# An even spread of the retention tiles over mixed weight chunks, and the rotation moved to VectorE

## What is computed

```python
h = rmsnorm(x, g_pre); proj = h @ w_in              # 1024 x 6144: q, k, v, gate
q = rope(q, pos); k = rope(k, pos) * 128 ** -0.5    # 8 heads: q, k of 128, v of 256
scores = einsum(q, k) * inner_dec; inner = scores @ v
R = R * g_c + (k * zeta).T @ v; cross = (q @ R) * xi  # a state carried along the tokens
o = group_norm(inner + cross) * gn_gain
y = (silu(gate) * o) @ w_out; out = x + rmsnorm(y, g_post)
```

## Time and profile before

| | us |
|---|---|
| median of 3 runs (2574.51 to 2578.9) | 2576.57 |
| the profiled execution | 2579.79 |
| its span | 2578.0 |
| first chunks 0 and 1 (14 products), from the start | 143.57 |
| end of the last projection product | 682.40 |
| first matmul of closing tile 2 | 799.41 |

### The profile page before, as it was taken

How to read it: one execution, slowest core, us unless ns; L and a number is a source line. 1 busy time by engine, 2 the same in 40 slices (tenths; PEclk the granted TensorE clock), 3 DMA queues, 4 the chain that set the end, 5 groups by cost and what they waited for, 6 DMA issues and landing times.

```text
span 2578.0 us, 33119 instructions
## 1 busy us (share of the span) xinstructions
PE 2416.0 (94%) x11720; PEld 2026.0 (79%) x11720; DVE 1634.3 (63%) x2643; ACT 1037.8 (40%) x1886; POOL 870.1 (34%) x764
## 2 busy tenths in 40 slices
PE   5599989998778999999999999999999999999999
PEld 4478777777656889878888888888888888888887
DVE  7344777888553244117776577867748766687775
ACT  3454433433331134245555454544434333333332
POOL 4647665665532222062222100110115232342212
PEclk8799999999888999999999999999999999999999
DMA  4333344433645351212233411112242443654422
GB/s 172 111 128 101 115 121 133 130 116 102 181 118 173 125 159 59 93 47 74 67 102 103 152 58 39 53 46 66 78 139 83 179 173 135 241 212 163 164 98 82
DMA packets 157131, 302.17 MB, mean 117 GB/s; under 512 B 13681, under 2 KB 83441, under 8 KB 155761
## 3 DMA queue, kind: packets, MB, share of 16 engines
q1 hardware_dynamic: 156976, 300.18, 35.1%
HBM read 207.07 MB, written 88.87 MB: 115 GB/s over the span
## 4 chain that ended last, share of the span: by engine, by line
PE 71%; DVE 13%; issue 6%; ACT 4%; DMA 2%; POOL 2%; SPq 1%; DVEq 0%; ACTq 0%; POOLq 0%
PE ff_ps L4341 11%; PE ff_ps L4368 10%; PE gl_vr_ps L2972 7%; PE wa_y_ps L503 6%; PE ra_apart_ps L1549 4%; PE ra_even_ps L1549 3%; PE wb_y_ps L3329 3%; PE gl_j_ps L2931 3%; PE la_x_ps L1766 3%; PE wc_y_ps L3710 3%; DVE ra_w_lower L1312 2%; PE ff_ps L4399 2%; PE ra_odd_ps L1549 1%; PE la_cq_ps L1705 1%; DVE ra_oS L1364 1%
## 5 line engine op out<-in xcount | busy, mean ns | idle before, releaser
L4368 PE MATMUL ff_ps<-ff_p,ff_p 128*128 128x512 f32 x1176 | 268.1, 390 | 0.8 <-issue 0.6
L4368 PEld LDWEIGHTS ff_ps<-ff_p,ff_p 128*128 128x128 f32 x1176 | 220.3, 188 | 48.6 <-issue 2.4
L1312 DVE TENSOR_TENSOR ra_w_lower<-ra_b,ra_w_upper 128x1024 fp32r<-128x1024 f32 x60 | 111.2, 1854 | 64.7 <-ACT ra_w_upper L869 64.3
L503 PE MATMUL wa_y_ps<-wa_wh,wa_gl 128*128 128x512 f32 x256 | 108.8, 425 | 31.6 <-POOL wa_wl L459 17.1
L2699 POOL TENSOR_SCALAR gl_mo<-gl_so 128x1 f32<-128x1 f32 x32 | 16.0, 501 | 332.4 <-ACT gl_osq L2637 332.4
L3987 ACT ACTIVATE ff_p<-ff_h 128x1024 fp32r<-128x1024 f32 x51 | 54.2, 1062 | 163.6 <-PE ff_ps L4368 163.6
L4212 DVE TENSOR_TENSOR ff_p<-ff_h,ff_p 128x1024 fp32r<-128x1024 f32 x51 | 80.7, 1582 | 42.7 <-ACT ff_p L3987 42.7
L503 PE MATMUL wa_y_ps<-wa_wh,wa_gh 128*128 128x512 f32 x256 | 105.1, 411 | 0.0
L503 PE MATMUL wa_y_ps<-wa_wl,wa_gh 128*128 128x512 f32 x256 | 105.0, 410 | 0.0
L1549 PE MATMUL ra_even_ps<-ra_s_upper,ra_w_lower 128*128 128x512 f32 x240 | 95.7, 399 | 9.2 <-DVE ra_s_lower L1300 9.2
L2972 PE MATMUL gl_vr_ps<-gl_vrh,x_lower 128*128 128x512 f32 x256 | 102.1, 399 | 0.0
(11 more groups left out here) (565 smaller groups left out, 7705.6 us busy)
## 6 DMA issues: line engine op xcount, KB each, us to landing
ff_h<-hidden SPq DMA_DIRECT2D x53, 512.0 KB, 3.4
ra_b<-in_w_chunks_a SPq DMA_DIRECT2D x48, 512.0 KB, 5.1
staging<-heads_a SPq DMA_DIRECT2D x64, 256.0 KB, 3.8
hidden<-ff_s SPq DMA_DIRECT2D x29, 512.0 KB, 2.8
ff_v<-in_w_ff SPq DMA_DIRECT2D x28, 512.0 KB, 6.9
ff_b<-in_w_ff SPq DMA_DIRECT2D x24, 512.0 KB, 6.1
hidden<-ff_a SPq DMA_DIRECT2D x24, 512.0 KB, 2.8
silu_a<-ra_c SPq DMA_DIRECT2D x16, 512.0 KB, 2.8
```

The lines of the kernel that those rows point to most:

```text
L503: last = pe.matmul(y_ps[slot][:, c, :], a[:, slot, kt, :], b[kt][:, c * HALF:(c + 1) * HALF], start=(kt == 0 and i == 0), stop=(kt == KW - ...
L1312: dve.tensor_tensor(lower[:, :, :], factor(c, p)[:, :, :], upper[:, :, :].bitcast(F32), ALU.subtract).then_inc(wl_done, 1)
L4368: end = pe.matmul(to[:, u, :], a[:, k, i * P:(i + 1) * P], b[:, k, :], start=(opens and p < 3 and k == 0 and m == 0), stop=(k == 1 and m = ...
```

## The change

Four things are changed together.

1. The weight columns are put in another order, so that chunks 0, 1, 2, 4, 5, 6, 8 and 9 are heads and 3, 7, 10 and 11 are gates. Chunks 0 and 1 go product by product in turns.
2. The 64 tiles stand at even distances from slot 32 (chunk 2) to slot 164 (chunk 11); a tile's attend step is always two slots behind its scores step, the deviation three, the normalisation five, the store six.
3. VectorE rotates: chunks 0 and 1 behind products 11 to 13 of the 14 opening ones, each later head at slots 4 and 12 of its chunk. GpSimd keeps the weight sums, the gates' scaling and the deviations. The scaling of x goes from GpSimd and VectorE to ScalarE, and all w_out rows are split by ScalarE and VectorE.
4. Each w_out row has a place of its own and is split where it lies; rows 0 to 7 are loaded during the last chunk. `LAG` goes from 2 to 4. The post gain is loaded after the rows. In the last closing tiles one x half waits for the fifteenth row in place of the twelfth (`XL_FREE`).

```diff
-    both = np.concatenate([gate, heads], axis=1)
+    gate, heads = gate.reshape(DM, -1, HALF), heads.reshape(DM, -1, HALF)
+    both = np.concatenate([heads[:, 0:3], gate[:, 0:1], heads[:, 3:6], gate[:, 1:2], heads[:, 6:8], gate[:, 2:4]], axis=1).reshape(DM, -1)
...
+    HEAD_CHUNKS = (0, 1, 2, 4, 5, 6, 8, 9)
+    GATE_CHUNKS = (3, 7, 10, 11)
...
-        FIRST = [(0, 0), (1, 0), (0, 1), (1, 1)] + [(c, p) for c in range(2) for p in range(2, PRODUCTS)]
-        FIRST += [(c, p) for c in range(2, CHUNKS) for p in range(PRODUCTS)]
+        FIRST = [(c, p) for p in range(PRODUCTS) for c in range(2)] + [(c, p) for c in range(2, CHUNKS) for p in range(PRODUCTS)]
...
-        SCORES_AT = {3: 0, 4: 1, 6: 2, 7: 3, 9: 4, 10: 5, 12: 6, 13: 7}
-        ATTEND_AT = {5: 0, 6: 1, 8: 2, 9: 3, 11: 4, 12: 5, 14: 6, 15: 7}
-        NORM_LATER = 4
-
-        def core_step(table, c, slot, later=0):
-
-            for h, key in ((c - GATES - 1, slot - later), (c - GATES - 2, slot + SLOTS - later)):
-                if 0 <= h < RET_HEADS and key in table:
-                    return h, table[key]
-            return None
+        OPENING, CLOSING = 2 * SLOTS + 4, CHUNKS * SLOTS - 4
+        SCORES_AT = [OPENING + (CLOSING - OPENING) * s // (LAST - 1) for s in range(LAST)]
+        TILE_AT = {at: divmod(s, NT) for s, at in enumerate(SCORES_AT)}
+        ATTEND, DEVIATE, NORM, STORE = 2, 3, 5, 6
+
+        def tile_at(c, slot, later=0):
+
+            return TILE_AT.get(SLOTS * c + slot - later)
...
-        ROW_AT = [8 * i for i in range(8)] + [80, 88, 96, 136, 144, 152, 104, 168]
-        LAG = 2
+        ROW_AT = [8 * i for i in range(8)] + [80, 88, 96, 152, 168, 144, 136, 104]
+        LAG = 4
...
-        EARLY = {(FINAL, 10): (0, 0), (FINAL, 12): (0, 1), (CHUNKS, 0): (1, 0), (CHUNKS, 1): (0, 2), (CHUNKS, 2): (1, 1),
-                 (CHUNKS, 3): (1, 2), (CHUNKS, 9): (0, 3), (CHUNKS, 11): (1, 3)}
-        G_ORDER = list(EARLY.values()) + [(t, q) for t in range(2, NT) for q in range(NQ)]
+        EARLY = {(FINAL, 8): ((0, 0),), (FINAL, 13): ((0, 1),), (CHUNKS, 0): ((0, 2),), (CHUNKS, 1): ((1, 0), (1, 1)),
+                 (CHUNKS, 2): ((1, 2),), (CHUNKS, 3): ((0, 3), (1, 3))}
+        PRODUCT_AT = {(FINAL, 11): ((0, 0),), (FINAL, 13): ((0, 1),), (CHUNKS, 0): ((0, 2),), (CHUNKS, 1): ((1, 0), (1, 1)),
+                      (CHUNKS, 2): ((1, 2),), (CHUNKS, 7): ((0, 3), (1, 3))}
+        G_ORDER = [key for keys in EARLY.values() for key in keys] + [(t, q) for t in range(2, NT) for q in range(NQ)]
...
+        def turn(eng, h, half, n, buffer, part, done):
+
+            c = HEAD_CHUNKS[h]
+            x_ = formed_of(c)[(C11, C21)[half]]
+            at = slice(half * HALF, (half + 1) * HALF)
+            eng.wait_ge(add_done, ADDS[c, 5 if half else 1] + 2)
+            eng.tensor_tensor(buffer[:, 0, :], x_[:, 1, :], sin[:, at], ALU.mult)
+            eng.tensor_tensor(buffer[:, 1, :], x_[:, 0, :], sin[:, at], ALU.mult).then_inc(part, 1)
+            eng.wait_ge(part, 3 * n + 1)
+            eng.tensor_tensor(x_[:, :, :], x_[:, :, :], cos[:, at].rearrange("p (a n) -> p a n", a=1).broadcast_to([P, 2, HALF]),
+                              ALU.mult).then_inc(part, 1)
+            eng.wait_ge(part, 3 * n + 2)
+            eng.tensor_tensor(x_[:, 0, :], x_[:, 0, :], buffer[:, 0, :], ALU.subtract).then_inc(part, 1)
+            eng.tensor_tensor(x_[:, 1, :], x_[:, 1, :], buffer[:, 1, :], ALU.add).then_inc(done, 1)
...
-                at = ROW_FROM[kt]
-                if row_use(kt) > 1:
-                    row_lowered(sp, max(k for k in range(kt) if ROW_FROM[k] == at))
-                elif at == 136:
-                    sp.wait_ge(wl_done, PLACE[FINAL, 0] + 1)
-                    sp.wait_ge(t_done, 4 * FINAL + 1)
-                elif at == 140:
-                    sp.wait_ge(wl_done, PLACE[FINAL, 2] + 1)
+                if kt < 8:
+                    sp.wait_ge(f_mm, 2 * PLACE[FINAL, 2 + kt // 2] + 2)
+                elif kt < 11 or kt == 15:
+                    sp.wait_ge(f_mm, 2 * PLACE[FINAL, 6] + 2)
+                elif kt == 12:
+                    wait_stored(sp, C22, FINAL)
+                    wait_stored(sp, C12, FINAL)
+                elif kt == 11:
+                    sp.wait_ge(gT_mm, G_PLACE[1, 3] + 1)
                 else:
-                    sp.wait_ge(turn_done, 2 * RET_HEADS)
-                sp.dma_start(row_slots[at][:, :], w[kt * P:(kt + 1) * P, :]).then_inc(row_in[at], 16)
+                    sp.wait_ge(gl_done, G_PLACE[kt - 13, 3] + 1)
+                if kt >= 8:
+                    sp.wait_ge(rows_h, kt - 7)
+                sp.dma_start(raw_rows[kt][:, :], w[kt * P:(kt + 1) * P, :]).then_inc(row_in[kt % 8], 16)
...
+            def scale_rows(x_, k):
+                for kt in range(KT // 2):
+                    last = act.activation(x_[:, kt, :], x_[:, kt, :], ACT.Copy, scale=gain_in[:, 4 * k + kt:4 * k + kt + 1])
+                last.then_inc(xg_done, 1)
...
+                if n == 11:
+                    dve.wait_ge(xrms_done, NT)
+                    dve.wait_ge(con_in, 48)
+                    dve.tensor_tensor(zr[:, :, :], xrms[:, 1:2, :].broadcast_to([P, RET_HEADS, NT]),
+                                      zeta[:, :].rearrange("p (h n) -> p h n", n=1).broadcast_to([P, RET_HEADS, NT]),
+                                      ALU.mult).then_inc(zr_done, 1)
+                    scale_turns(0)
+                    rotate(0, 0)
+                if n == 12:
+                    rotate_odd(0)
+                    scale_turns(1)
+                if n == 13:
+                    rotate(0, 1)
+                    rotate_odd(1)
...
+                    core(c, 2 * p + j)
+                    if c >= 2 and c in HEAD_CHUNKS and 2 * p + j in (4, 12):
+                        rotate(HEAD_CHUNKS.index(c), p // 6)
...
+            for c in range(2, CHUNKS + 1):
+                head = HEAD_CHUNKS.index(c) if c in HEAD_CHUNKS else None
+                for slot in range(SLOTS if c < CHUNKS else TAIL):
+                    if slot == 0 and c < CHUNKS:
+                        sum_of(c, T4)
+                    if slot == 0 and c - 1 in GATE_CHUNKS:
+                        scale_gates(c - 1, 3)
+                    if at := tile_at(c, slot, DEVIATE):
+                        deviation(*at)
+                    if c < CHUNKS:
+                        if slot == 4 and head is None:
+                            scale_gates(c, 0)
+                        if slot == 6 and c < FINAL:
+                            sum_of(c + 1, T1)
+                        if slot == 10 and head is None:
+                            scale_gates(c, 1)
+                        if slot == 11 and c < FINAL:
+                            sum_of(c + 1, T3)
+                            sum_of(c + 1, T2)
+                        if slot == 12 and head is None:
+                            scale_gates(c, 2)
+                    for at in PRODUCT_AT.get((c, slot), ()):
+                        g_lower(pool, *at)
...
+            for c in range(2, CHUNKS):
+                own = HEAD_CHUNKS.index(c) if c in HEAD_CHUNKS else None
+                last = HEAD_CHUNKS.index(c - 1) if c - 1 in HEAD_CHUNKS else None
+                for slot in range(SLOTS):
+                    core(c, slot)
+                    if c > 2 and last is not None:
+                        if slot == 0:
+                            store_values(last, 0)
+                        if slot == 2:
+                            store_turned(last, 1)
+                    elif c > 2:
+                        if slot == 2:
+                            store_gates(c - 1, C21)
+                        if slot == 4:
+                            store_gates(c - 1, C12)
+                    if c < FINAL and slot in (1, 3, 7, 9):
+                        load_raw(c + 1, {1: B11, 3: B12, 7: B21, 9: B22}[slot])
+                    if own is not None:
+                        if slot == 8:
+                            store_turned(own, 0)
+                        if slot == 10:
+                            store_values(own, 1)
```

## The result

The changed kernel takes 2490.61 us (median of 4 runs, 2488.93 to 2493.78) against 2576.35: a ratio of 0.9668, 95% interval 0.9651 to 0.9685. The forecast was 2481 with a range of 2445 to 2532. The gain is 85.7 us by the medians where 95.4 were forecast. Of the 9.6 between 2481 and 2490.6, 5.0 are in the sum (90.9 measured between the two profiled executions, 2579.79 and 2488.93, against 95.9).

A forecast was written before the change was run, and what follows sets the result against it. It took TensorE and VectorE as level in the chunks (48.5 against 48.1 us). Opening 112, ten chunks 532 and tail 58 gave 702 against 799.4; the gain less 1.5 was 95.9, so 2481 us, range 2445 to 2532.

The forecast's parts named there:

- The opening without the rotation: Start of the kernel up to chunk 2, before adding the rotated halves: 106 us, against 143.6 before the change.
- the wait of 22.1: TensorE's 22.1 us wait in the opening for a block of the gates; claimed to go, since gates no longer stand there.
- The backlog of four halves: Four rotated halves on VectorE behind opening products 11 to 13, 15.7 us of work: 6 us put on the path.
- the tail: After the ten chunks, up to closing tile 2's first matmul: 58 us, between 50 and 85, against 117.0 before.
- The period: Time of each of ten chunks after the opening: 53.2 us, from 48.5 floor, 1.4 for Rl and 3.3 half clock.
- The floor: TensorE's own work per chunk after the opening: 48.5 us, from 38.1 for products plus 6.4 tiles at 1.63.
- The wait for ra_oS (5.4) goes: TensorE's 5.4 us per chunk waiting for the previous tile's output copy vanishes, as attend steps stand two slots apart.
- The price of a half: One rotated half on VectorE, four instructions of 0.68 and one of 1.21: 3.9 us.
- The hold: VectorE held by GpSimd's sums and gate scalings in the ten chunks: 12.5 us a chunk at 0.42, 5.2.
- my sign for ql and sTl: Expected in the trace after: mean times of VectorE's ql and sTl instructions nearer to 0.28 us than to 0.77.
- The rival of VectorE as the bound: In the ten chunks GpSimd's hold and dearer rotation make VectorE the limit: period 57.5, time 2524 us, chance 0.16.
- the slower rival: SP's one queue loads weight blocks late behind stores of rotated halves, making the kernel slower than before; chance 0.04.

## Why the prediction was right, and where its steps failed

The opening without the rotation was put at 106. Chunk 2 begins at 105.4 in the changed kernel and at 103.7 in the one without any rotation, and the wait of 22.1 went: right as a sum. Its parts were not, and that they cancel is luck: the splits of x took 1.4 where I kept 6 and the additions 6.1 where I kept 8, and 3.7 went to lower halves of weights, which the sum does not have. This was read from the traces; no experiment put the gates first again. The backlog of four halves was put at 6 (between 0 and 15.7) and costs 15.8 by the kernel without them: the upper bound. I took 6 because VectorE has time beside a product; it has none there, because the scale row comes at 99 us and puts all four behind it, into chunk 2's first products.

By the traces the 8.8 us between 702 and 710.8 come apart like this: the opening without rotation 103.7 for 106, the backlog 14.0 for 6, the ten chunks without the backlog 538.2 for 532, the tail 54.9 for 58. (The backlog is taken from the two kernels without the later rotation.)

The period was put at 53.2 and is 55.05. Of the 18.5 us in ten periods 10.9 are chunk 2's alone (64.1); the other nine chunks take 54.0 each. The floor was right, and can be counted: 485 for ten chunks. What TensorE's busy time of 502.1 has above it, 17, is half clock, 1.7 a chunk where I kept 3.3 (the granted clock is 0.97 over the ten chunks, so by an estimate some 33 of the 550 us ran at the lower of its two levels, 1.2 in place of 2.4 GHz). The waits are 5.1 a chunk where I kept 1.4. The step that failed is "The wait for ra_oS (5.4) goes": 2.2 a chunk are left of it, and VectorE's additions have 2.0 (half of that is the one wait of 10.2 in chunk 2). I had looked at the distance of two attend steps and not at what makes the copy late. The copy is the last link of a chain that begins on VectorE, and VectorE was put level with TensorE (48.1 against 48.5) and then given no lateness. The two errors, 1.6 too much half clock and 3.7 too little waiting, partly cancelled. (A slip in the range: a period of 51 is 22 us under the forecast for ten chunks, 2459 and not 2457. Nothing rests on it.)

The price of a half, 3.9, is right for an undisturbed one (4.0 without sums) and low for one among sums (5.4). The hold was put at 5.2 a chunk. Against their undisturbed durations ql, sTl and Rl lost 45.6 - 64 x 0.28 = 27.7, 38.0 - 64 x 0.28 = 20.1 and 31.5 - 56 x 0.43 = 7.4, and the twelve halves 12 x 1.4 = 17: 7.2 a chunk, without the opening's. Why 5.2 was too little can be read in the kernel before: its 0.42 counts ql, Rl and sTl, and in the chunk that it was taken from two more were held, the normalisation (5.7 - 8 x 0.40 = 2.5) and the weights' lower halves (9.0 - 6 x 1.22 = 1.7):

```profile
L1364 DVE TENSOR_SCALAR ra_oS<-ra_oS,ra_mv,ra_rstd 128x256 f32<-128x256 f32 x8 | 5.7, 710 | 0.0
L1312 DVE TENSOR_TENSOR ra_w_lower<-ra_b,ra_w_upper 128x1024 fp32r<-128x1024 f32 x6 | 9.0, 1495 | 0.3 <-ACT ra_w_upper L869 0.3
```

With them it is 15.2 of 26.1, 0.58, and 12.5 x 0.58 = 7.2. The cost of a tile would have been 3.5 with it in place of 4.0, and VectorE's sum 46.9 in place of 48.1: this error did not make the forecast too low. So my sign for ql and sTl, means nearer to 0.28 than to 0.77, was wrong: 0.71 and 0.59. The hold did not go with GpSimd's rotation, it moved to the rotation itself and stayed on the tiles.

The rival of VectorE as the bound had a chance of 0.16 and 2524 us, from a period of 57.5. The mechanism is this rival's, at under half its size (the period is 1.9 over the forecast's 53.2, the rival's 4.3): VectorE decides the last 3.5 to 3.9 us of a period (550.5 against 515.5 and 511.7 for ten), TensorE the rest. What the Trainium skill says there (Perfetto Trace Analysis, section "Optimizing Scalar/DVE Operations"), that it may make sense to take work off a saturated VectorE, points the right way for the six later heads and the wrong way for the opening (2474.2 against 2493.7); its other half, that a move between GpSimd and VectorE may not help, agrees with 54 of 65 us coming back as hold.

The tail was put at 58 and takes 54.9: the rows' waits went entirely. The 1.5 for the later x half did not show; behind closing tile 2 the profiled execution gained 2.3 more, and why was not tried. Which of the tail's edits did how much was not tried either. SP (the slower rival) is named once in the changed kernel, with 3.0 for the first tile's load, and with 14.9 for the same load in the kernel with head 1 on GpSimd. The mechanism of that rival, a load behind a store that waits for a rotation, is there in the opening of the changed kernel: chunk 2's last weight block is issued at 110.5, behind the store of head 1's first half (109.1), and GpSimd's sums, which wait 31.1 us for it, then hold the fourth rotated half.

## What to carry to other kernels

When two engines come out level, TensorE's floor and a helper's load, put the waits of TensorE at several us a period (here 5.1) and not at nothing, and look at the longest block on the helper's list in front of an instruction on the chain. A wait is named after its last link: before counting it as gone, follow it back to the engine that was late. And between GpSimd and VectorE count work together with the hold it makes on the other; moving the rotation left VectorE's busy time within 11 of 445 us, and what changed the time was in part the arrangement. Where the work stands decided as well: on GpSimd the later heads' rotation saved 16.4 us, and the opening's lost 19.5.

## What the runs showed of the hardware

The hold works both ways and for whole instructions: a sum of 2.39 us took 3.12 when it began during VectorE's product, and VectorE's 0.69 then took 2.77. It also reaches an instruction with one tensor in SBUF, which I had left out of the hold: the normalisation's mean rose from 0.433 to 0.609 with the rotation on GpSimd, at a median of 0.404. Here is one of them, with the GpSimd product that held it until 246.90:

```profile
244.57 2.48 DVE L1363 TENSOR_SCALAR ra_oS<-ra_oS,ra_mv,ra_rstd 128x256 f32<-128x256 f32 x1
243.64 3.26 POOL L500 TENSOR_TENSOR ra_c<-ra_c,ra_cos 128x1024 f32<-128x1024 f32 x1
```

The additions, which read one block in PSUM and one in SBUF, were not held in the changed kernel (minimum, median and maximum in ns):

```profile
L1277 DVE TENSOR_TENSOR ra_c<-ra_apart_ps,ra_c x66: 671/683/692, 41.9 to 652.5; 128x512 f32<-128x512 f32 x66
```

How much of GpSimd's time becomes VectorE's loss depends on what is counted. Over ql, sTl and Rl alone it was 0.42 before the change and 0.33 for the rotation put back ((16.9 + 5.9 + 11.0) / 101). Over all instructions it was 0.58 and 0.53.
